# A two-block transformer kernel: the decay of its gated linear attention moved early and split by head, its low-rank rows in four row groups, and twenty projection chunks cut from 528 to 514 tokens

## The reference

```
# block 1 (528 tokens)
q_a, k_a, v_a, f_a, q_b, k_b, v_b, g_a, g_b = split(rms_norm(h) @ w_in)
o_a = forgetting_attention(q_a, k_a, v_a, log_sigmoid(f_a + b_forget))     # 8 heads of 64
o_b = stick_breaking_attention(q_b, k_b, v_b)                              # 8 heads of 64
mixed = (sigmoid(g_a) * (o_a @ w_o_fox) + sigmoid(g_b) * (o_b @ w_o_sb)) @ w_out
h = h + rms_norm(mixed)
h = h + rms_norm(gelu_gated(causal_depthwise_conv(rms_norm(h) @ w_up)) @ w_down)   # conv width 3
return h[:, 16:]

# block 2 (512 tokens): swiglu, hybrid mixer, swiglu, gated projection, final norm
gq, gk, gv, gr, ga, dq, dkv, iq, ik, iw, gates = split(u @ w_in)
log_a = log_sigmoid(ga @ alpha_w + alpha_b) / 16        # ga: 16 low-rank features; 4 heads x 128
# gla_chunked, for each of 4 heads (dk 128, dv 256) in chunks of 64 tokens:
b = cumsum(log_a)
scores[t, s] = sum_d q[t, d] * k[s, d] * exp(b[t, d] - b[s, d])            # s <= t
o = scores @ v + (q * exp(b)) @ state
y_gla = (rms_norm(o) * silu(gr)) @ gla_w_out
c_kv = rms_norm(dkv)                                     # the other branch: a top-k attention
y_dsa = dsa_attention(dq, c_kv, iq, ik, iw, rel_bias) @ dsa_w_out
h = h + (sigmoid(g_gla) * y_gla + sigmoid(g_dsa) * y_dsa) @ w_out
```

## Time and profile before

| | |
|---|---|
| median of 3 runs | 2201.43 us (2199.3 to 2204.84) |
| profiled execution: its own time, its span | 2204.3 us, 2202.4 us |
| mean granted TensorE clock | 0.993 |
| PE busy | 2158.6 us (98%), 12472 instructions |
| PEld | 1855.5 us (84%) |
| DVE | 992.6 us (45%) |
| ACT | 753.0 us (34%) |
| POOL | 1005.0 us (46%) |
| chain that ended last, by engine | PE 82%, issue 7%, DVE 5%, POOL 4%, ACT 1% |
| weight transfers | 170 of 1024 KB, 4.8 us each to landing |

### The profile page before, as it was taken

How to read it: one execution, slowest core, us unless ns; L and a number is a source line. 1 busy time by engine, 2 the same in 40 slices (tenths; PEclk the granted TensorE clock), 3 DMA queues, 4 the chain that set the end, 5 groups by cost and what they waited for, 6 DMA issues and landing times.

```text
span 2202.4 us, 31272 instructions
## 1 busy us (share of the span) xinstructions
PE 2158.6 (98%) x12472; PEld 1855.5 (84%) x12472; DVE 992.6 (45%) x1451; ACT 753.0 (34%) x1003; POOL 1005.0 (46%) x812
## 2 busy tenths in 40 slices
PE   8999999989999999999999999999999999999998
PEld 7897999989999887888888777878777888888886
DVE  5244454279888208322201618671875452322017
ACT  4133455343222216222213324552336332222134
POOL 4322223455555547555544543254331555555444
PEclk9999999999999999999999998999999999999999
DMA  4321111212222323222222221024220223222222
GB/s 163 101 73 63 58 59 58 97 58 96 95 95 82 113 100 113 99 95 97 93 105 93 104 90 56 20 77 137 93 77 20 83 91 111 90 103 96 95 97 95
DMA packets 31837, 194.94 MB, mean 89 GB/s; under 512 B 3968, under 2 KB 4480, under 8 KB 9984
## 3 DMA queue, kind: packets, MB, share of 16 engines
q1 hardware_dynamic: 26352, 182.66, 23.3%
q10 hardware_dynamic: 5392, 10.95, 1.5%
HBM read 189.24 MB, written 4.23 MB: 88 GB/s over the span
## 4 chain that ended last, share of the span: by engine, by line
PE 82%; issue 7%; DVE 5%; POOL 4%; ACT 1%; DMA 0%; SPq 0%; DVEq 0%; POOLq 0%; ACTq 0%
PE ps L2207 72%; POOL wlo L664 4%; PE ps L2757 2%; PE ps L2865 1%; DVE sqa L1437 1%; PE ps L2892 1%; PE ps L2975 1%; PE ps L2949 1%; DVE x2lo L1425 1%; ACT whi L727 1%; PE ps L2486 0%; PE ps L2509 0%; PE ps L2930 0%; PE ps L2545 0%; DMA h<-h 0%
## 5 line engine op out<-in xcount | busy, mean ns | idle before, releaser
L664 POOL TENSOR_TENSOR wlo<-raw,whi 128x512 fp32r<-128x512 f32 (+2 forms) x808 | 1004.8, 1275 | 1174.1 <-ACT whi L727 1078.1
L727 ACT CAST whi<-raw 128x2048 fp32r<-128x2048 f32 x165 | 315.2, 1910 | 822.0 <-PE ps L2207 764.3
L2207 PE MATMUL ps<-x2hi,whi 128*128 128x512 f32 x1136 | 450.1, 396 | 1.2 <-DVE x2lo L1425 1.1
L2207 PE MATMUL ps<-x2hi,wlo 128*128 128x512 f32 x1136 | 443.6, 391 | 0.0
L2207 PE MATMUL ps<-x2lo,whi 128*128 128x512 f32 x1136 | 443.5, 390 | 0.0
L2207 PE MATMUL ps<-xhi,whi 128*128 128x256 f32 x1344 | 276.5, 287 | 21.4 <-DVE xlo L1490 9.6
L2207 PE MATMUL ps<-xlo,whi 128*128 128x256 f32 x1344 | 273.4, 285 | 0.0
L2207 PE MATMUL ps<-xhi,wlo 128*128 128x256 f32 x1344 | 273.2, 285 | 0.0
L2207 PEld LDWEIGHTS ps<-x2hi,whi 128*128 128x128 f32 x1136 | 214.1, 188 | 50.1 <-issue 5.3
L2207 PEld LDWEIGHTS ps<-x2hi,wlo 128*128 128x128 f32 x1136 | 214.1, 188 | 45.1
L2207 PEld LDWEIGHTS ps<-x2lo,whi 128*128 128x128 f32 x1136 | 214.2, 189 | 44.0 <-issue 1.4
(11 more groups left out here) (442 smaller groups left out, 2741.1 us busy)
## 6 DMA issues: line engine op xcount, KB each, us to landing
raw<-wstream SPq DMA_DIRECT2D x170, 1024.0 KB, 4.8
h<-h SPq DMA_DIRECT2D x4, 528.0 KB, 8.5
ncb<-c_rows ACTq DMA_DIRECT2D x8, 256.0 KB, 3.5
ple_rows<-ple_out ACTq DMA_DIRECT2D x4, 512.0 KB, 4.0
bias<-bias_rows ACTq DMA_DIRECT2D x8, 256.0 KB, 4.5
ple<-ple_rows ACTq DMA_DIRECT2D x4, 512.0 KB, 5.4
out_dram<-outb SPq DMA_DIRECT2D x8, 256.0 KB, 2.8
raw<-wstream ACTq DMA_DIRECT2D x4, 256.0 KB, 7.3
```

The source lines that it names most:

```text
L664: return nc.gpsimd.tensor_tensor(wlo[b][:, cols], raw[b][:, cols], whi[b][:, cols].bitcast(F32), ALU.subtract)
L727: nc.scalar.copy(whi[b][:], raw[b][:]).then_inc(sig("hi_done"), 1)
L2207: ins = mm(dst, w[slot][:, cols], xx(tok), start=first and p_ == 0, stop=last and p_ == 2, skip_group_check=True)
```

## The change

- **514 tokens.** The four query chunks of the second attention and the sixteen gate chunks are computed, emptied and, for the gates, put through the sigmoid on tokens 14 to 527 only. The first 14 columns of the queries are set to zero once.
- **Row groups.** alpha_w is loaded in four transfers, the part of head hd on rows 32 x hd; the low-rank rows are copied by three transfers from `narrow` to rows 0, 32 and 64 of a new tile, and stay on rows 96 and on for the fourth head. The four alpha products (and the turns of iw ahead of them) move between the sixth and the seventh tile of the dkv chunk, and go to banks 5, 6, 7 and 1.
- **Decay.** Head 0's goes all the way at once, ahead of the loop. The others' linear part, sum and cumulative sum are in loop turns 1, 4 and 5 (head 1), 14 (head 2) and 23 (head 3). nb_ready counts heads. ckv's refinement and multiplication go to turn 3, the copy of its turned tile to turn 7, the turn itself on PE to q = 6, its sum of squares to bank 4.
- **Order of the filling.** Only 16 gr tiles stand ahead of the loop and 48 in it, by a new list. The cast of U_GR + 1 goes behind head 0's exponent and logarithm; U_GR + 2 is cast by quarters in turns 1 and 2, U_GR + 3 in 9 to 12, U_MG1 in 22, 23, 24 and 26; gr chunks leave PSUM in the loop. ik_low's transfer is issued at q = 5.
- **Places.** ax, restart, gf2 and negs lie elsewhere in memory.

The diff, cut to its core:

```
+        def first_of(d):
+            return SKIP if D_QKB <= d < D_QKB + 4 or d >= D_GATES else 0
...
+        GR_IN_STEP = (1, 3, 3, 3, 3, 3, 1, 1, 2, 2, 1, 1, 0, 0, 1, 1, 1, 2, 1, 1, 1, 0, 0, 1, 1, 1, 2, 1, 1, 1, 0,
+                      1, 1, 2, 2, 2)
         def gr_tiles_by(q):
-            i, part = (q - 1) // 9, (q - 1) % 9
-            return 8 * i + (0, 0, 1, 2, 3, 4, 5, 6, 8)[part]
+            return UT + sum(GR_IN_STEP[:q])
...
# ACT
-                    nc.scalar.activation(gates[:, c, :], gates[:, c, :], ACT.Sigmoid).then_inc(sig("gate_on"), 1)
+                    used = gates[:, c, SKIP:T1]
+                    nc.scalar.activation(used, used, ACT.Sigmoid).then_inc(sig("gate_on"), 1)
...
-            act.dma_start(aw[GA], alpha_w).then_inc(sig("aux_in"), 16)
+            for hd in range(4):
+                rows, cols = slice(32 * hd, 32 * hd + META), slice(hd * P, (hd + 1) * P)
+                act.dma_start(aw[rows, cols], alpha_w[:, cols]).then_inc(sig("aux_in"), 16)
...
+            act.wait_ge(sig("narrow_out"), 1)
+            for hd in range(3):
+                act.dma_start(low_rank[32 * hd:32 * hd + META], narrow[GA]).then_inc(sig("aux_in"), 16)
+            def decay(part, heads):
+                act.wait_ge(sig("decay_x"), part)
+                step.up(nc.scalar.activation(al[:, heads], al[:, heads], ACT.Exp))
+                step.wait()
+                nc.scalar.activation(al[:, heads], al[:, heads], ACT.Ln, bias=one_col).then_inc(sig("decay_ln"), 1)
+            act.wait_ge(sig("brow_out"), 16)
+            decay(1, slice(0, 1))
+            hi_of(U_GR + 1)
             act.wait_ge(sig("evac2"), U_GR - U_GQK)
             nc.scalar.activation(sq[0][:, 0:SEQ], dkvf[:], ACT.Square).then_inc(sig("ckv_sq"), 1)
+            decay(2, slice(1, 4))
...
+                if 1 <= q <= NG + 1:
+                    for c in gr_chunks_after(q - 1):
+                        gr_out(c, False)
+                if q in (1, 2):
+                    hi_quarter(U_GR + 2, 2 * q - 2)
+                    hi_quarter(U_GR + 2, 2 * q - 1)
+                if q == 5:
+                    act.wait_ge(sig("ckv_ready"), 1)
+                    act.dma_start(ik_low[64:P], narrow[0:64]).then_inc(sig("ik_in"), 16)
+                if 9 <= q <= 12:
+                    hi_quarter(U_GR + 3, q - 9)
+                if q in (22, 23, 24, 26):
+                    hi_quarter(U_MG1, min(q - 22, 3))
...
# DVE
-                return regions[:, STAGE1[d][0] // 2, LO:LO + T1]
+                return regions[:, STAGE1[d][0] // 2, LO:LO + T1 - first_of(d)]
...
+            step.up(vec.memset(qkb[:, 0:4, 0:SKIP], 0.0))
...
+            decay_in(head0)
+            decay_in(others)
+            dve.wait_ge(sig("unit_done"), U_SPC + 1)
+            vec.tensor_copy(dkvf[:], bank(4)).then_inc(sig("evac2"), 1)
+            decay_ramp(head0, 1)
+            decay_out(head0, 1)
+            decay_sum(0)
+            vec.tensor_scalar(iwt, bank(0)[:, 0:32], ...).then_inc(sig("iw_ready"), 1)
+            for q in range(NG + 2):
+                if q == 1:
+                    decay_ramp(others, 2)
+                if q == 3:
+                    scale = refined(bank(4), 1.0 / P)
+                    dve.wait_ge(sig("evac2"), U_GR - U_GQK)
+                    vec.scalar_tensor_tensor(out=ckvf[:], ...).then_inc(sig("ckv_ready"), 1)
+                if q == 4:
+                    decay_out(others, 2)
+                if q == 5:
+                    decay_sum(1)
+                if q == 7:
                     dve.wait_ge(sig("ckv_turned"), 1)
                     step.up(vec.tensor_copy(ckvt[:].rearrange("p j c -> p (j c)"), bank(4)))
+                if q in (14, 23):
+                    decay_sum(q // 9 + 1)
...
# PE
+                    if c == 0 and k == 5:
+                        pe.wait_ge(sig("narrow_out"), 1)
+                        pe.wait_ge(sig("aux_in"), 176)
+                        pe.wait_ge(sig("evac2"), 8)
+                        pe.wait_ge(sig("gv_ready"), 4)
+                        ...
+                        for hd in range(4):
+                            rows = slice(32 * hd, 32 * hd + META)
+                            mm(alpha_bank(hd), aw[rows, hd * P:(hd + 1) * P], (low_rank if hd < 3 else narrow)[rows],
+                               start=True, stop=True).then_inc(sig("alpha_done"), 1)
...
             gr_tiles(0, KC)
             pe.wait_ge(sig("ckv_sq"), 1)
-            mm(bank(1), one_col.to_broadcast([P, P]), sq[0][:, 0:SEQ], start=True, stop=True
+            mm(bank(4), one_col.to_broadcast([P, P]), sq[0][:, 0:SEQ], start=True, stop=True
...
             gr_tiles(KC, UT)
-            pe.wait_ge(sig("decay_x"), 1)
-            gr_tiles(UT, UT + KC)
...
-            gr_tiles(UT + KC, 2 * UT)
+            pe.wait_ge(sig("decay_x"), 2)
             pe.wait_ge(sig("iw_ready"), 1)
             for q in range(1, NG + 4):
                 if q <= NG:
-                    gr_tiles(2 * UT + gr_tiles_by(q - 1) if q > 1 else 2 * UT, 2 * UT + gr_tiles_by(q))
+                    gr_tiles(gr_tiles_by(q - 1), gr_tiles_by(q))
+                if q == 6:
+                    pe.wait_ge(sig("ckv_ready"), 1)
...
```

More of the change, by code:

```diff
@@ L1134, in _ @@
             act.dma_start(scratch.ap(), brow[:]).then_inc(sig("brow_out"), 16)
-            for u in range(U_GV, U_GR):
+            for u in range(U_GV, U_GR - 1):
                 hi_of(u + 2)
+            nc.scalar.preload_act_table_set("natural_log_exp_and_others")
+            act.wait_ge(sig("narrow_out"), 1)
[9 more added lines that the diff above has]
+            hi_of(U_GR + 1)
             act.wait_ge(sig("evac2"), U_GR - U_GQK)
-            nc.scalar.preload_act_table_set("natural_log_exp_and_others")
             nc.scalar.activation(sq[0][:, 0:SEQ], dkvf[:], ACT.Square).then_inc(sig("ckv_sq"), 1)
+            decay(2, slice(1, 4))
             act.wait_ge(sig("ckv_sums"), 1)
-            rsqrt_of(bank(1), 1.0 / P)
+            rsqrt_of(bank(4), 1.0 / P)
             gr_out(0)
[L1145 to L1155, removed]
             for q in range(NG + 4):
@@ L1960, in _, with decay_in @@
             step.up(vec.memset(restart[:].rearrange("p (j c) -> p j c", c=P)[:, :, 0:1], 0.0))
-            dve.wait_ge(sig("decay_ln"), 1)
-            step.up(vec.scalar_tensor_tensor(out=ax[:], in0=al[:], scalar=1.0 / 16, in1=ax[:],
-                                             op0=ALU.mult, op1=ALU.add))
-            step.wait()
-            for hd in range(4):
-                if hd == 3:
+            def decay_in(heads):
+                for hd in range(heads.start, heads.stop):
+                    dve.wait_ge(sig("alpha_done"), hd + 1)
+                    step.up(vec.tensor_scalar(ax[:, hd, :], alpha_bank(hd), cv[:, C_AB + hd:C_AB + hd + 1], None,
+                                              ALU.add))
+                step.wait()
+                vec.scalar_tensor_tensor(out=al[:, heads], in0=ax[:, heads], scalar=-1.0, in1=ax[:, heads],
+                                         op0=ALU.mult, op1=ALU.min).then_inc(sig("decay_x"), 1)
@@ new lines, in decay_ramp, with decay_out @@
+            def decay_ramp(heads, part):
+                dve.wait_ge(sig("decay_x"), part)
+                step.up(vec.tensor_scalar(ax[:, heads], ax[:, heads], -1.0 / 16, 0.0, ALU.mult, ALU.max))
+            def decay_out(heads, part):
+                dve.wait_ge(sig("decay_ln"), part)
+                step.wait()
+                step.up(vec.scalar_tensor_tensor(out=ax[:, heads], in0=al[:, heads], scalar=1.0 / 16,
+                                                 in1=ax[:, heads], op0=ALU.mult, op1=ALU.add))
```

91 lines of the change are left out of this document (38 added, 53 removed).

## The result

The changed kernel takes 2210.29 us (median of 7 executions, 2209.5 to 2213.12) against 2203.14 of the kernel before beside it (7, 2198.87 to 2204.84): ratio 1.0042, 95% interval 1.0032 to 1.0051. It is slower by a little more than what a measurement can tell from no change. 2201.1 was forecast, with a range of 2190 to 2209.

A forecast was written before the change was run, and what follows sets the result against it. The prediction took PE's work and waits, including a half-clock stretch in head 0, as the bound. Gains of 18.6 us less 12.6 of new waits and 5.7 of clock gave 0.3 less: 2201.1 us, range 2190 to 2209.

The forecast's parts named there:

- rival "slower": Clock falls after both heads' fourth step, staying low (7.9 us each), plus 4 us in head 0: 2215; chance 0.15.
- idle ahead of head 0's first masked step: PE's two idle stretches there, 0.8 and 2.66 us, go because head 0's decay is ready early: 3.5 us gained.
- lower clock of head 0: Half-clock stretch behind head 0's idle time, priced by comparing heads 0 and 1, goes: 7.9 us gained.
- alpha products: The four products and small transposes, 3.6 us, overlap in four row groups: 2.3 us gained.
- waits at the first masked steps, heads 1 to 3, and one later: Short waits for gf there go, as new tiles stand ahead of those first masked steps: 2.8 us gained.
- the low-rank copies: PE's wait for three copied row sets ahead of the alpha products: 0 to 1.2 us, taken as 0.2.
- head 0, second masked step and the next two: PE waits while DVE refines ckv beside POOL's pieces, 4.2 us, then 0.45 in each of two turns: 5.1 added.
- heads 1 and 2, fourth masked step: Next head's scan delays DVE's factors with no tile beside it: waits of 2.95 us twice, 5.9 added.
- new stretches at the lower clock: New waits lower PE's clock in head 0 (2.2 us) and one of heads 1 and 2 (3.5): 5.7 lost.
- the toll of POOL: At head 0's second masked step, POOL's four pieces lengthen DVE's two-input operations by 1.03 us each, three or four times.
- the last step: Net saving of 0.3 us subtracted from both the profiled execution (2204.3) and the median (2201.43): 2204.0 and 2201.1.
- rival "the clock holds": New waits in the heads bring no lower clock: 2201.4 - 6.0 = 2195.4 us; chance 0.30.

The follow-up runs named there:

- experiment 3: Changed kernel with ckv's refinement and multiplication in loop turn 2 instead of 3: 2207.88 us, ratio 1.0028 to the kernel before.
- experiment 6: Experiment 1's kernel with POOL's subtraction for U_GR + 2 in sixteen pieces of 128 columns instead of four of 512: 2203.59 us, ratio 1.0011.
- experiment 1: Changed kernel with the weight load issued ahead of the third low-rank copy held until the copies have landed: 2205.44 us, ratio 1.0015.
- experiment 5: Experiment 4's kernel with dense tiles moved from turns 11, 12, 20, 21 to 13, 14, 22, 23, head 3's likewise: 2196.84 us, ratio 0.9983.
- experiment 11: Early-alpha kernel of experiment 9 with two scans and tiles moved (2189.02 us), plus two dead scans each at turns 14 and 23: 2196.89 us, ratio 0.9982.
- experiment 2: Changed kernel with the scans of heads 2 and 3 one turn earlier, in 13 and 22: 2205.37 us, ratio 1.0017.
- experiment 4: Changed kernel with the edits of experiments 1, 2 and 3 together: 2199.43 us, ratio 0.9991.
- experiment 7: Changed kernel with the row groups undone: one alpha_w transfer, no low-rank copies, alpha products one after another: 2209.43 us, ratio 1.0034.
- experiment 9: Kernel before with 514 tokens, row-grouped alpha products behind the dkv chunk, load behind copies, all decay ahead of the loop: 2192.33 us, ratio 0.9970.

## Why the prediction was wrong

The kernel came out slower, as the rival "slower" had it, which had 0.15, but not at that rival's price: the clock fell in both heads and cost 4.4 and 3.1 us there, not 7.9 each. The rest is a term of the forecast that was sized too small, and a base that did not fit.

| step of the prediction | forecast, us | the two profiles, us |
|---|---|---|
| idle ahead of head 0's first masked step | -3.5 | -3.5 |
| lower clock of head 0 | -7.9 | -7.9 |
| alpha products | -2.3 | -2.4 |
| 514 tokens | -2.1 | -2.5 |
| waits at the first masked steps, heads 1 to 3, and one later | -2.8 | -2.6 |
| the low-rank copies | +0.2 | +3.1, and 1.6 by the clock |
| head 0, second masked step and the next two | +5.1 | +4.5 |
| heads 1 and 2, fourth masked step | +5.9 (2.95 twice) | +5.9 (3.44 + 2.46) |
| head 3 and smaller ones | +1.4 | +0.4 |
| new stretches at the lower clock | +5.7 | +9.7 |
| sum | -0.3 | +6.3, measured +5.8 |

- **What was right.** The new waits in the loop came where they were worked out. Head 0's has the forecast size and cause, the toll of POOL (4.2 forecast at the second masked step, 4.52 measured; experiments 3 and 6). The 5.9 of heads 1 and 2 is right by luck: head 2's wait is 0.5 shorter than forecast and head 1's 0.5 longer, by a second toll of POOL that the prediction did not have. The gains of the row groups and of head 0's early decay are there.
- **The first step that failed** is the wait for the low-rank copies, "0 to 1.2, I take 0.2". Issue times and landing were right for the first two. The text named the weight load issued at the same moment and gave it 1.2 us at most; experiment 1 shows it cost 3.1 of wait, and 4.9 with the clock. The third copy landed when the 1 MB ahead of it had landed, and the row for that, 4.8 us for a weight load, stood on the page.
- **The second** is the clock, "I take head 0 and one of the other two: 5.7". It fell in head 0 (2.2 lost as forecast), in both others (4.4 and 3.1) and behind the copies. The step that priced one head was a compromise between two cases; the nearest rows (a fall behind 2.66 us of idle time) spoke for both. A wait of this size does not bring it down each time (experiments 5 and 11), but the changed kernel has four such waits, and all seven executions of it are at 0.990 or 0.991.
- **The third** is the base, the last step: "the sum gives 2204.0 for it and 2201.1 for the median". The 7.9 us credited for head 0's clock are of an execution with a clock of 0.993, at 2204.3; in 36 of 75 the kernel before has 0.995 or more and is 4 to 5 us faster. The median of three shown, 2201.43, lay between, so part of that gain was never in it, and the sum held for the profiled execution alone. Of the 9.2 us between 2201.1 and 2210.29 these are 2.9; 6.1 are the difference of the two profiles, +5.8 for -0.3.
- **A slip in the chances** changed nothing in the forecast: the rival "the clock holds", at 2195.4, was counted as below 2194.8.

Open: which activity exactly makes the clock fall. The same wait of 1.2 us kept and lost it (experiments 2 and 4), and so did one of 3.1 us at the same place (experiments 5 and 4), waits of 2.1 us lost it in seven executions of ten by their times, and 3.6 us of products on few rows lost it without a wait (experiment 7). That these products are the cause there is argued from their place alone. That POOL's pieces are what holds DVE's operations is shown by their sizes changing together; by which mechanism is not.

## What to carry to other kernels

Ask of each small transfer that the critical engine waits for which large one goes out just before it, and price it at that one's landing. Count a new wait of 2 us or more on TensorE among short products about twice (waits of 4.52, 3.44 and 2.46 us cost 2.2, 4.4 and 3.1 more by the clock here), and look in several executions at the granted clock before crediting a gain to it. Work added to an in-order queue belongs where the other engine is busy with long work that needs nothing of it: the scan was 1.3 us of a wait in turn 14 and none in turn 13, beside the output products. The decay ahead of the loop, started 8 us earlier (experiment 9: the alpha products at 1309.5 for 1318.1), needed no place in the loop to be faster than both kernels, and with two scans in such turns and other places for the tiles it was faster still.

## What the runs showed of the hardware that was not expected

- A copy of 32 KB took 2.0 us to land, and 5.0 when 1 MB had been issued 0.2 us before on another engine's queue.
- A VectorE operation of 256 columns with two SBUF inputs took 1.48 us beside GpSimd's subtractions of 512 columns, 0.68 beside those of 128 and 0.41 alone; the whole subtraction took GpSimd 12.2 us in the small pieces against 6.5.
- TensorE's granted clock fell behind 3.6 us of 16-row products without any idle time, and one and the same program kept it in some executions and lost it in others.
